# Moving operands of the input projection, second output projection, gate and up at 192 and 64 modulo 256 bytes, in a one-core float32 decoder step

## The reference, cut to what matters

```
z = rms_norm(x) @ w_in                     # 2048 -> 4352
x = x + rms_norm(concat(oA, oB) @ w_out)   # 1024 + 1024 -> 2048
h = rms_norm(x)
u, up = h @ w_gate, h @ w_up               # 2048 -> 5632 each
y = (gelu(conv3(u)) * up) @ w_down         # 5632 -> 2048
x = x + rms_norm(y)
```

## The kernel before

| operand | before | with the change |
|---|---|---|
| `wh`, `wl`, every 128 x 128 block | 128 | 128 |
| `hh` rows (high parts: input, gate, up) | 128 | 192 |
| `hl` rows (low parts: input, gate, up) | 128 | 64 |
| second output projection, high / low | 128 / 128 | 192 / 64 |
| `oBh`, `oBl` row j | 224 + 32 j | 224 + 32 j |
| `gh` row kt / `gl` row kt | 128 + 32 kt / 32 kt | 128 + 32 kt / 32 kt |
| `ysq`, `yT` (over `hh`, `hl`) | 128, 128 | 192, 64 |
| all tensors of the attention and feed-forward parts | | the same as before |

## Time and profile before

### The profile page before, as it was taken

The page is one execution under the profiler, slowest core; times in us unless marked ns, Lnnn a source line. Parts: engine busy times, 40 slices in busy tenths (PEclk is TensorE's granted clock), DMA queues, the critical chain, the costliest instruction groups (busy, mean ns, idle before and its releaser), DMA issues.

```text
span 1174.4 us, 25613 instructions
## 1 busy us (share of the span) xinstructions
PE 1156.3 (98%) x9985; PEld 1123.8 (96%) x9985; DVE 700.8 (60%) x1055; ACT 553.1 (47%) x859; POOL 104.1 (9%) x162
## 2 busy tenths in 40 slices
PE   9999999999999999999999999999999999999995
PEld 8999889988999899999999999999999999999994
DVE  6877565674475976565656556565656444454445
ACT  7545555565455754454444444444444333343331
POOL 0100111111011010010011001000100000020001
PEclk9999999999999999999999999999999999999998
DMA  9646676667545355555555555545555655555542
GB/s 336 191 151 228 236 254 238 214 226 246 176 160 191 105 177 181 204 168 190 176 183 185 170 200 176 192 161 201 174 183 191 199 180 179 180 180 180 182 154 74
DMA packets 60499, 222.24 MB, mean 189 GB/s; under 512 B 7064, under 2 KB 9312, under 8 KB 58336
## 3 DMA queue, kind: packets, MB, share of 16 engines
q1 hardware_dynamic: 56032, 196.53, 50.2%
q0 software_dynamic: 4272, 24.94, 6.3%
q10 hardware_dynamic: 144, 0.05, 0.0%
HBM read 216.45 MB, written 5.00 MB: 189 GB/s over the span
## 4 chain that ended last, share of the span: by engine, by line
PE 92%; DVE 5%; ACT 2%; DMA 1%; issue 0%; SPq 0%; DVEq 0%
PE ps L1188 29%; PE ps L1189 28%; PE ps L1190 28%; DVE wl L706 1%; PE ps L1361 1%; PE ps L1279 1%; PE ps L1342 1%; PE ps L1270 1%; DMA raw<-in_w_in 1%; PE ps L1268 1%; PE ps L1297 0%; DVE yT L1035 0%; PE ps L1215 0%; DVE ps L1034 0%; PE ps L1462 0%
## 5 line engine op out<-in xcount | busy, mean ns | idle before, releaser
L1188 PE MATMUL ps<-hh,wh 128*128 128x264 f32 x2048 | 583.2, 285 | 1.7 <-DVE wl L878 1.1
L1190 PE MATMUL ps<-hh,wl 128*128 128x264 f32 x2048 | 576.6, 282 | 0.0
L706 DVE TENSOR_TENSOR wl<-raw,wh 128x1024 fp32r<-128x1024 f32 x363 | 438.3, 1225 | 182.4 <-ACT wh L426 181.9
L1189 PE MATMUL ps<-hl,wh 128*128 128x264 f32 x1920 | 540.6, 282 | 0.0
L426 ACT CAST wh<-raw 128x1024 fp32r<-128x1024 f32 x363 | 374.4, 1046 | 262.5 <-PE ps L1190 259.5
L1188 PEld LDWEIGHTS ps<-hh,wh 128*128 128x128 f32 x2048 | 383.7, 187 | 12.7 <-issue 11.2
L1190 PEld LDWEIGHTS ps<-hh,wl 128*128 128x128 f32 x2048 | 383.7, 187 | 0.0
L1189 PEld LDWEIGHTS ps<-hl,wh 128*128 128x128 f32 x1920 | 359.8, 187 | 0.1
L1189 PE MATMUL ps<-gl,wh 128*128 (+1 forms) x704 | 200.4, 285 | 0.0
L1188 PE MATMUL ps<-gh,wh 128*128 (+1 forms) x704 | 200.1, 284 | 0.0
L1190 PE MATMUL ps<-gh,wl 128*128 (+1 forms) x704 | 199.5, 283 | 0.0
(11 more groups left out here) (246 smaller groups left out, 896.7 us busy)
## 6 DMA issues: line engine op xcount, KB each, us to landing
raw<-in_w_gate SPq DMA_DIRECT2D x88, 512.0 KB, 3.7
raw<-in_w_up SPq DMA_DIRECT2D x88, 512.0 KB, 4.5
raw<-in_w_down SPq DMA_DIRECT2D x88, 512.0 KB, 3.5
raw<-in_w_in SPq DMA_DIRECT2D x67, 512.0 KB, 4.6
raw<-in_w_out SPq DMA_DIRECT2D x32, 512.0 KB, 3.6
Kt<-in_kb POOLq DMA_DIRECT2D x8, 1284.0 KB, 6.1
Vk<-in_vb POOLq DMA_DIRECT2D x8, 1024.0 KB, 6.8
out_y<-yT SPq DMA_DIRECT2D x8, 264.0 KB, 2.3
```

The source lines that it names most:

```text
L706: V.tensor_tensor(wl[:, slot], raw[:, slot], wh[:, slot].bitcast(F32), ALU.subtract).then_inc(lo_ready, 1)
L1188: nc.tensor.matmul(out, a, x, start=start, stop=False)
L1189: nc.tensor.matmul(out, a, xl, start=False, stop=False)
L1190: return nc.tensor.matmul(out, b, x, start=False, stop=stop)
```

## The change

It moves two buffers by a few bytes and adds nothing. The spacer before `hh` grows from 16 to 32 floats (`hh` +64 bytes), a new spacer of 32 floats stands before `hl` (+128 bytes more), and a third of 16 floats after it brings all later tensors to a shift of exactly 256 bytes. The second output projection's low parts go 32 floats into their rows (128 bytes). No instruction is added, removed or reordered.

```
-        sb("align", [P, 16])
+        sb("align", [P, 32])
         with ExitStack() as over:
-            hh = sb("hh", [P, MT, ROW], F32R, over)[:, :, 0:TOK]
+            rows = sb("hh", [P, MT, ROW], F32R, over)
+        hh = rows[:, :, 0:TOK]
+        o2h, o2l = hh[:, 0:OT], rows[:, OT:2 * OT, 32:32 + TOK]
         ysq = sb("ysq", [P, MT, ROW])[:, :, 0:TOK]
 
+        sb("align_l", [P, 32])
         with ExitStack() as over:
             hl = sb("hl", [P, MT, ROW], F32R, over)[:, :, 0:TOK]
         yT = sb("yT", [P, MT, ROW])[:, :, 0:TOK]
+        sb("align_a", [P, 16])
...
-                        dst = hh[:, j] if X else oBh[:, j]
+                        dst = o2h[:, j] if X else oBh[:, j]
...
-                        hi, lo = (hh[:, j], hh[:, OT + j]) if X else (oBh[:, j], oBl[:, j])
+                        hi, lo = (o2h[:, j], o2l[:, j]) if X else (oBh[:, j], oBl[:, j])
...
-                    gemm(chunk(B_OUTB, i, 4, 2 * g + c), 2 * ((G_IN + G_OUT + g) % 2), hh, hh[:, OT:2 * OT],
+                    gemm(chunk(B_OUTB, i, 4, 2 * g + c), 2 * ((G_IN + G_OUT + g) % 2), o2h, o2l,
...
-                        ins = mm3(ps[:, bank, 0:TOK], (slot, 256 * k + P * m), hh[:, 4 * c + k], hh[:, OT + 4 * c + k],
+                        ins = mm3(ps[:, bank, 0:TOK], (slot, 256 * k + P * m), o2h[:, 4 * c + k], o2l[:, 4 * c + k],
```

## The result

| | before | with the change |
|---|---|---|
| median of 21 runs each | 1176.19 us | 1182.44 us |
| lowest to highest | 1175.12 to 1184.70 us | 1181.73 to 1183.32 us |
| ratio, 95% interval | | 1.0044 [1.0034, 1.0054] |
| span of the profiled execution | 1174.4 us | 1180.6 us |

A forecast was written before the change was run, and what follows sets the result against it. The number of matmuls times the distance of their starts was taken to bound the kernel. Input projection -1.1 us, all else 0, gave 1175.1 us profiled, median 1174.8; likeliest case 1173 to 1175.5, range up to 1181.5.

The forecast's parts named there:

- What bounds the kernel: Whole kernel: the span is the number of matmuls times the distance between starts; only changing that distance can pay.
- Gate and up, "the difference is 0": Gate and up, 1,408 triples: 360 ns each before and after, difference 0, with bounds of +9.9 and -4.2 us.
- always from the same predecessor: Down: a caveat that kt 26 settles within two triples, though it is always entered from kt 25.
- the forecast 0.57: Likeliest case, chance 0.57: gate and up unchanged, input projection a little better, 1173 to 1175.5 us.
- The rival "slower": Gate and up lose their even pace: +4 ns a triple gives 1180.4 us, +7 ns 1184.7; chance 0.17.
- is even from there on: Gate, first turn: after the sums of squares, 128 and 128 becomes even at 120 ns from 410.32 us.
- this pair has two paces: 128 and 128 was said to have an even pace of 120.0 ns and an uneven one of 121.3.
- Input projection, -1.1 us: Input projection, 544 triples: 1.5 us gained from an even pace less 0.4 us for settling, net -1.1 us.
- The 1.5 us "to be had": Input projection: two thirds of 1,632 matmuls gain 1.33 ns each if the new pair is always even.
- the rival "no change": The new pair is uneven as often as the old between breaks, 1175.9 us; no change or small loss, chance 0.17.
- Second output projection, 0: Second output projection, 128 triples: one even pair to another, 0, with bounds of +0.9 and -0.4 us.
- That addresses are indifferent: All stages: by the rule of two independent read ports no start address matters, sum 0, 1175.9 us; no separate chance.

The follow-up runs named there:

- experiment 2: The kernel before with one small matmul ahead of each of the 20 looped gate-and-up turns; 1183.22 us, one run.
- experiment 8: The kernel before with one small matmul after chunk 1 of gate's second turn; five runs from 1176.25 to 1177.04 us, five from 1181.36 to 1183.04.
- experiment 1: The changed kernel with one small matmul ahead of each of the 20 looped gate-and-up turns; 1181.54 us, one run.
- experiment 3: The changed kernel with one small matmul after chunk 1 of gate's second turn; 1176.64 us, ratio to the kernel before 0.9999.
- experiment 7: The changed kernel with the second output projection's operands back at 128 and 128; 1182.50 us.
- experiment 6: The kernel before with high and low parts at 0 modulo 256 in input projection, second output projection, gate and up; 1191.72 us, ratio 1.0110.
- experiment 10: The kernel before with weights and both parts of those stages' moving operands 64 bytes further, at 192 modulo 256; 1181.19 us, one run.
- experiment 5: The kernel before with high parts at 128, low parts at 160 in input projection, second output projection, gate and up; 1176.30 us, ratio 0.9978.

## Why the prediction was wrong

*What bounds the kernel: right.* The number of matmuls times the distance of their starts gives the loss: 4,007 distances x 1.48 ns = 5.9 us of the 6.2 us by which the span grew.

*Gate and up, "the difference is 0": wrong, and this is the step that failed.* I took the settled part of kt 26 as the pace of 192 and 64. It is one of at least two. What I had seen was not many samples: each passage of that pair in down comes in from the pair of kt 25 in the same way, and all six of them in the first half of down (kt 2, 10, 18, 26, 34, 42) have the same 24 distances within 1 ns. The trace repeats one draw. I wrote down that it settles "always from the same predecessor" and still gave the forecast 0.57. The kernel before had shown how to weigh it: 128 and 128 was uneven in about two thirds of the input projection (23 of 61 stretches between breaks were even, by their last twelve distances). A pair of which only one draw is known should have had odds near a half for the slow side.

*The rival "slower": right in mechanism and price, with the wrong break.* It named a pace like the uneven one, picked by a break and held, and +4 ns a triple; measured are 364.4 against 360 ns. But the break of the earlier trace rows is not the last. I wrote that the stream "is even from there on" and held for 490 us; it is broken twice more, in the kernel before by the last sums of squares and by the sum L1485 at 419.47 us:

```profile
415.45 1.10 PE L1215 MATMUL ps<-sqx,ones 128*32 128x264 f32 x16
416.48 0.39 PE L1188 MATMUL ps<-hh,wh 128*128 128x264 f32 x1
```

From 416.83 to 419.47 us the pace is a third one of 128 and 128, 122 120 116 122 ns in turn, with a mean of 120.0 again; so the sentence that this pair has two paces falls short too. The rival gave 1180.4, since it was laid on top of an input projection better by 1.1 us, which did not come; without that it would have been 1181.5. The 0.4 ns a triple by which it was short add 0.6 us, and the second output projection 0.4: 1182.5 us, about as measured. Its chance of 0.17 was the fault, and so was a range cut off at 1181.5.

*Input projection, -1.1 us: wrong.* 192 and 64 was even in 28 of 61 stretches, hardly more than the 23 before, and its uneven pace is as slow: the mean of the distances that are no breaks went from 120.99 to 120.89 ns, and the stage, from the first matmul to the first output projection, from 276.2 to 276.1 us. Other traces of the same input projection vary by more than that: 27 and 29 of 61 at 128 and 128 (experiments 2 and 8), 25, 22 and 25 at 192 and 64 (experiments 1, 3 and 7). Its L1193 is recorded at 284 ns, not nearer to 281. The 1.5 us "to be had" assumed that the new pair is always even. That was the rival "no change", right for this stage.

*Second output projection, 0: slightly wrong,* +0.45 us, inside the bound of +0.9: its stretches, one of 310 distances among them, drew the uneven pace, 121.5 ns.

*Down, first output projection, attention, 0: right.* 259.97 and 259.93 us for down, and kt 26 takes 2.887 us in both. That the remainder modulo 256 is what counts held.

*That addresses are indifferent: not borne out.* This was the rival that the Trainium skill's sentence on two independent read ports (TensorE: Matmul & The Clock Gate, step 4 of "Step-by-step: what each phase is for") stands behind. The same instructions take 15 us more with other addresses alone (experiment 6), and the paces followed the distance from moving operand to weights in the one shift tried (experiment 10).

What stays open: why the changed kernel's break draws the uneven pace in all of its 21 runs, while the kernel before splits 16 to 5 there. The traces show where they part. The first three rows are one program up to 423 us; so are the four traces of the last row, but for the second output projection of experiment 7:

| stretch that begins at about | 392 us | 410 us | 417 us | 420 us |
|---|---|---|---|---|
| 128 and 128: kernel before | uneven | even | even | even |
| the same, experiment 2 | even | uneven | uneven | even |
| the same, experiment 8 | uneven | uneven | even | uneven |
| 192 and 64: the changed kernel, experiments 1, 3 and 7 | uneven | uneven | even | uneven |

At 192 and 64 four traces of four go through the same paces, even where the second output projection had other addresses. At 128 and 128 no two traces agree, and the same pace is followed by different ones: after the break at 408 us uneven becomes even in one trace and stays uneven in another. So what a break does is not fixed by the pace before it alone at these places, other than at the small matmuls of experiment 2; what else enters was not isolated. That the upper heap of the kernel before is the uneven pace in gate and up is inferred from its size (4,007 x 1.33 ns = 5.3 us), from experiment 10 and from the uneven stretch ahead of the small matmul in experiment 8, since no run of that heap was itself profiled. Why a given distance between starts gives these patterns, no run tells.

## What to carry to other kernels

A long unbroken stream of matmuls ran here at several paces with the same addresses, 0.9 to 2.8% apart, and the last break ahead of it, together with what stood before, decided which. Before a layout is judged by a run, look at the distances in its longest stretches and at whether its runs fall in heaps; one small matmul at the entry of the stretch, which cost 0.2 us here, makes a new draw. An address pair that looks good in a trace must be seen to settle from several different entries before it is counted on.

## What the runs showed that I had not expected

- One added 128-column matmul made the changed kernel 5.8 us faster (experiment 3).
- With the same small matmul ahead of each turn, 128 and 128 alternates strictly between its two paces, and 192 and 64 takes the even one 20 times in 20.
- 120.0 ns for 264 columns is the lowest lasting mean in all twelve traces, whatever the addresses (no 48 distances in a row average under 119.8), though single distances go down to 115 ns.
- Shifting weights and moving operands together by 64 bytes reproduces both patterns within 1 ns (experiment 10).
- A pair can need some 16 matmuls to settle (experiment 5), so a mean over a chunk of 24 can mistake the settling for a pace.
